# Expert gates scattered into a DRAM table by indirect transfers, in place of a one-hot gate stage

## What is computed

```python
q = (h @ w_q).reshape(B, L, PEER_HEADS, 2, PEER_HALF)
s = jnp.einsum('blhpd,pnd->blhpn', q, sub_keys).astype(jnp.float32)
top_s, top_i = lax.top_k(s, PEER_TOPK)
cand_s = top_s[..., 0, :, None] + top_s[..., 1, None, :]
cand_i = top_i[..., 0, :, None] * PEER_NKEYS + top_i[..., 1, None, :]
best_s, best_pos = lax.top_k(cand_s.reshape(B, L, PEER_HEADS, PEER_TOPK * PEER_TOPK), PEER_TOPK)
idx = jnp.take_along_axis(cand_i.reshape(B, L, PEER_HEADS, PEER_TOPK * PEER_TOPK), best_pos, axis=-1)
gate = jax.nn.softmax(best_s, axis=-1)
...
act = jax.nn.gelu(jnp.einsum('bpd,bphkd->bphk', hb, u).astype(jnp.float32), approximate=False)
coef = (act * gb).astype(hb.dtype)
return jnp.einsum('bphk,bphkd->bpd', coef, v_tab[ib])
```

## Time and profile before

| | us |
|---|---|
| median of 3 runs | 2644.88 |
| lowest, highest | 2641.59, 2645.89 |
| profiled execution | 2653.0 |
| its span, first to last instruction | 2651.1 |
| TensorE busy in the span | 2427.9 |
| VectorE busy | 1689.4 |
| ScalarE busy | 1294.4 |
| GpSimd busy | 0.4 |

### The profile page before, as it was taken

How to read it: one execution, slowest core, us unless ns; L and a number is a source line. 1 busy time by engine, 2 the same in 40 slices (tenths; PEclk the granted TensorE clock), 3 DMA queues, 4 the chain that set the end, 5 groups by cost and what they waited for, 6 DMA issues and landing times.

```text
span 2651.1 us, 47498 instructions
## 1 busy us (share of the span) xinstructions
PE 2427.9 (92%) x15508; PEld 2160.0 (81%) x15508; DVE 1689.4 (64%) x3506; ACT 1294.4 (49%) x2816; POOL 0.4 (0%) x5
## 2 busy tenths in 40 slices
PE   7989979999995799999899999989999985899998
PEld 2767779999995688888677778789999985788887
DVE  2565247888759766666225674238888769766665
ACT  1456145555558655554123422045555568655554
POOL 0000000000000000000000000000000000000000
PEclk9989989999999999999899899999999999999999
DMA  6445444555540255555332212445555530355554
GB/s 229 137 167 190 141 154 145 182 182 181 185 141 0 80 190 189 190 190 174 99 127 88 80 56 80 135 143 177 182 181 182 183 111 0 115 186 184 188 183 141
DMA packets 108500, 388.91 MB, mean 147 GB/s; under 512 B 12784, under 2 KB 15088, under 8 KB 107776
## 3 DMA queue, kind: packets, MB, share of 16 engines
q1 hardware_dynamic: 104256, 380.16, 43.1%
q10 hardware_dynamic: 4160, 7.61, 0.9%
HBM read 386.67 MB, written 1.05 MB: 146 GB/s over the span
## 4 chain that ended last, share of the span: by engine, by line
PE 83%; DVE 10%; issue 3%; ACT 2%; DVEq 0%; DMA 0%; ACTq 0%; PEld 0%; PEldq 0%
PE ps L707 19%; PE ps L1314 18%; PE ps L1308 11%; PE ps L1309 10%; PE ps L1310 10%; PE ps L1315 9%; DVE gbuf L1545 2%; DVE arena L1579 2%; PE ps L789 2%; PE ps L1000 1%; PE ps L978 1%; PE ps L1345 1%; DVE gbuf L801 0%; DMA ring<-stream 0%; PE ps L1570 0%
## 5 line engine op out<-in xcount | busy, mean ns | idle before, releaser
L1314 PE MATMUL ps<-csplit,hl 128*128 128x512 f32 x2048 | 721.2, 398 | 6.2 <-DVE hl L1611 6.2
L1308 PE MATMUL ps<-hsplit,hl 128*128 128x256 f32 x2304 | 656.3, 285 | 31.7 <-DVE hl L1385 31.7
L1309 PE MATMUL ps<-hsplit,hl 128*128 128x256 f32 x2304 | 655.5, 285 | 0.0
L1310 PE MATMUL ps<-hsplit,hl 128*128 128x256 f32 x2304 | 655.4, 284 | 0.0
L1315 PE MATMUL ps<-csplit,hl 128*128 128x256 f32 x2048 | 573.2, 280 | 0.0
L1382 ACT CAST hl<-ring 128x512 fp32r<-128x512 f32 x576 | 355.9, 621 | 388.0 <-PE ps L1310 387.7
L1385 DVE TENSOR_TENSOR hl<-ring,hl 128x512 fp32r<-128x512 f32 x576 | 397.6, 692 | 221.9 <-ACT hl L1382 189.8
L1308 PEld LDWEIGHTS ps<-hsplit,hl 128*128 128x128 f32 x2304 | 445.8, 193 | 32.8 <-ACT hl L1382 32.8
L1314 PEld LDWEIGHTS ps<-csplit,hl 128*128 128x128 f32 x2048 | 386.5, 189 | 99.6 <-issue 6.5
L707 PE MATMUL ps<-arena,ring 128*128 128x256 f32 (+2 forms) x1896 | 449.3, 397 | 15.5 <-issue 10.8
L1309 PEld LDWEIGHTS ps<-hsplit,hl 128*128 128x128 f32 x2304 | 445.7, 193 | 0.0
(11 more groups left out here) (194 smaller groups left out, 1808.7 us busy)
## 6 DMA issues: line engine op xcount, KB each, us to landing
ring<-stream SPq DMA_DIRECT2D x723, 512.0 KB, 3.3
arena<-keys ACTq DMA_DIRECT2D x2, 1024.0 KB, 4.9
gbuf<-consts ACTq DMA_DIRECT2D x1, 1120.0 KB, 5.1
arena<-xT ACTq DMA_DIRECT2D x1, 1024.0 KB, 10.3
arena<-ctxT ACTq DMA_DIRECT2D x1, 1024.0 KB, 12.7
resid<-xT ACTq DMA_DIRECT2D x1, 1024.0 KB, 8.8
out<-resid SPq DMA_DIRECT2D x1, 1024.0 KB, 3.9
gbuf<-consts ACTq DMA_DIRECT2D x1, 832.0 KB, 6.6
```

Of the source, the lines that this page charges most:

```text
L1308: pe.matmul(out_ap, w[0], m[0], start=start, stop=False)
L1309: pe.matmul(out_ap, w[1], m[0], start=False, stop=False)
L1310: return pe.matmul(out_ap, w[0], m[1], start=False, stop=stop)
L1314: pe.matmul(ps[:, bank, :], w_hi, m_both, start=start, stop=False)
```

## The change

The gates go through a table in DRAM, `gates_dram[b]`, laid out as (expert of the unit, unit, token) so that one cell of 4 bytes holds the gate of one expert and token; a unit's 128 x 256 gates are one contiguous 128 KB tile.

ScalarE's queue fills each table with zeros by 16 stores (`act_zero`): the first table's after the first norm, ahead of `con1` and `resid`, the second's ahead of the first expert layer, behind the keys. VectorE's work is regrouped in four rounds of four items. While it searches for round i, it also does the lookups and the softmax of round i - 1 (`lookup_part`, 14 steps), and ends with the numbers of the table's cells (`picks_at`). Several copies of the search are dropped, since the results are written in place. GpSimd then adds the gates into the table (`pool_scatter`): one accumulating indirect DMA for each of 256 columns of 128 tokens, with a wait for all that were sent before each head, as two heads of a token can pick the same expert.

The transposes on TensorE and the gate stage are gone. In the second-table stage SyncE loads the gate tile of a unit into `gring` (four slots), after it has waited once for all scatters, and VectorE multiplies the activations of a unit by it, two units ahead of use (`multiply`). The second table's stage starts on PSUM banks 4 to 7 while ScalarE still takes the last two units out of the others. The loops of the first-table stage are written out on VectorE and ScalarE. TensorE's loop has four units throughout.

```diff
+    gring, _ = place("gring", [P, GRING, T])
+    zeros, _ = place("zeros", [P, ZEROS])
...
+    gates_dram = {b: nc.dram_tensor(f"gates{b}", (P, P, T), F32, kind="Internal").ap() for b in (1, 2)}
...
+    hit = gring[:, :, :].rearrange("p r (c a) -> p (r c) a", a=TOPK)
...
         if n == 0:
-            eng.tensor_copy(keybuf[:, :], s_area[:, ds(i * 1024 + q * 256, 256)])
-            eng.drain()
-            for x, keys, _ in halves_of:
+            for x, keys, _ in both:
                 eng.max(topbuf[:, x, 0:8], keys)
...
         if n == 5:
-            eng.tensor_copy(index_f[:, :, ds(at, TOPK)], idxbuf[:, :, :])
...
         if n == 6:
-            eng.max(bestbuf[:, 0:8], keybuf[:, :])
-            eng.drain()
-            eng.match_replace(tmpbuf[:, :], bestbuf[:, 0:8], keybuf[:, :], NEG)
+            eng.max(best[:, at], keybuf[:, :])
         if n == 7:
-            eng.max(bestbuf[:, 8:16], tmpbuf[:, :])
-            eng.max_index(posbuf[:, 0:8], bestbuf[:, 0:8], keybuf[:, :])
+            eng.max_index(picks_pos[:, at], best[:, at], keybuf[:, :])
+            eng.match_replace(tmpbuf[:, :], best[:, at], keybuf[:, :], NEG)
...
         if n == 9:
-            eng.tensor_copy(sum_best[:, ds(at, TOPK)], bestbuf[:, :])
-            eng.tensor_copy(sum_pos[:, ds(at, TOPK)], posbuf[:, :])
+            eng.max_index(picks_pos[:, at8], best[:, at8], tmpbuf[:, :])
...
+    EXP_LAG = 3
+    def lookup_part(eng, b, i, n):
...
+        done = 4 * (b - 1) + i + 1
         if n == 0:
...
+            eng.tensor_copy(pos_f, picks_pos[:, :])
+            eng.tensor_copy(key_f, picks_key[:, :, :])
+            eng.tensor_tensor(g4, best, best[:, :, 0:1].broadcast_to([P, ITEMS, TOPK]), ALU.subtract)\
+               .then_inc(S("gates_shifted"), 1)
         if n == 1:
...
+            eng.tensor_scalar(rank1, pos_f, 1.0 / TOPK, -15.0 / 32, ALU.mult, ALU.add)
...
+        if 4 <= n < 10:
+            x, step = divmod(n - 4, 3)
...
             if step == 0:
...
+                eng.tensor_tensor(hit, rank, every, ALU.is_equal)
...
+                keys = key_f[:, x, :].rearrange("p (h o a) -> p h o a", h=ITEMS, o=1)\
...
+                eng.tensor_tensor(h4, h4, keys, ALU.mult)
             if step == 2:
...
+                eng.tensor_reduce(chosen[:, x, :], hit, AX_X, ALU.add)
+        if n == 10:
+            eng.wait_ge(S("gates_exp"), done)
+            eng.tensor_reduce(gate_sum[:, 0, :], g4, AX_X, ALU.add)
+            eng.scalar_tensor_tensor(chosen[:, 0, :], chosen[:, 1, :], float(P), chosen[:, 0, :], ALU.mult, ALU.add)
...
+            eng.scalar_tensor_tensor(chosen[:, 0, :], chosen[:, 0, :], float(T), c_("token"), ALU.mult, ALU.add)
...
+            eng.tensor_tensor(g4, g4, z, ALU.mult)
+        if n == 13:
+            eng.tensor_copy(picks_at[:, i, :], chosen[:, 0, :]).then_inc(S("picks_ready"), 1)
+        eng.drain()
...
+    def pool_scatter(pool, b):
+        cells = gates_dram[b].rearrange("j i (t o) -> (j i t) o", o=1)
+        pool.wait_ge(S(f"zeroed{b}"), 16 * (P * T // ZEROS // 4))
+        sent = (b - 1) * NT * HEADS * TOPK
+        for i in range(ROUNDS):
+            pool.wait_ge(S("picks_ready"), 4 * (b - 1) + i + 1)
+            for head in range(ITEMS // 2):
+                wait(pool, "scattered", 16 * sent)
+                for k in range(TOPK):
+                    for t in range(NT):
+                        c = (2 * head + t) * TOPK + k
+                        pool.indirect_dma_start(
+                            out=cells, out_offset=bass.IndirectOffsetOnAxis(ap=picks_at[:, i, c:c + 1], axis=0),
+                            in_=gates[:, i, c:c + 1], in_offset=None, compute_op=ALU.add,
+                            bounds_check=P * P * T - 1, oob_is_err=True).then_inc(S("scattered"), 16)
+                        sent += 1
+    def act_zero(act, b):
+        rows = gates_dram[b].rearrange("j i t -> j (i t)")
+        wide = zeros[:, :].rearrange("p (o n) -> p o n", o=1).broadcast_to([P, 4, ZEROS])
+        act.wait_ge(S("zeros_ready"), 1)
+        for n in range(P * T // ZEROS // 4):
+            act.dma_start(rows[:, n * 4 * ZEROS:(n + 1) * 4 * ZEROS].rearrange("j (o n) -> j o n", o=4), wide)\
+               .then_inc(S(f"zeroed{b}"), 16)
...
+    V_BANKS = (4, 5, 6, 7, 3, 0, 1, 2)
...
+    def multiply(dve, b, i, s):
+        at = s % GRING
+        dve.wait_ge(S(f"gates_in{at}"), i * 16 + 16 * ((b - 1) * N_IT + s // GRING + 1))
+        c = ds(i * (UB * T) + s * T, T)
+        dve.tensor_tensor(acts[:, c], acts[:, c], gring[:, at, :], ALU.mult).then_inc(S("gated"), 1)
...
+                        eng.copy(hl[:, hslot, 0, :], slot(unit)[:, part]).then_inc(S("split_hi"), 1)
                         if half == 0:
+                            eng.wait_ge(S("gated"), i * UB + ((b - 1) * P + s + 1))
                             eng.copy(csplit[:, cslot, 0, :], acts[:, c]).then_inc(S("csplit_hi"), 1)
-                        eng.copy(hl[:, hslot, 0, :], slot(unit)[:, part]).then_inc(S("split_hi"), 1)
...
+                        if first and s == 0 and half == 1:
+                            eng.wait_ge(S("u_bank_free"), banks_freed(b + 1, "wq"))
...
+                            mm = wide_passes(eng, v_bank(half * KD // 2 + n), w[0], w[1], csplit[:, cslot, :, :],
...
+                if kind == "act" and first and s == 0:
+                    take_unit(eng, b, 0, P - 2)
+                    take_unit(eng, b, 0, P - 1)
+                if kind == "dve" and not (last and s >= UB - 2):
+                    if first:
+                        eng.wait_ge(S("u_bank_free"), banks_freed(b, "u") + 4 + s + 3)
+                    elif last or s == 0:
+                        eng.wait_ge(S("u_bank_free"), banks_freed(b + 1, "wq"))
+                    multiply(eng, b, i, s + 2)
...
+        if kind == "dve":
+            for s in range(2):
+                eng.wait_ge(S("u_bank_free"), banks_freed(b, "u") + 4 + s + 1)
+                multiply(eng, b, 0, s)
...
-        with pe.Fori(0, TOPK_IT) as i:
-            for s in range(TOPK_UB):
-                u_unit("pe", pe, b, i, s, TOPK_UB)
-        for n in range(MID_UNITS):
-            u_unit("pe", pe, b, 0, MID_AT + n)
-            pe_gate_part(pe, b, n)
-        u_loop("pe", pe, b, MID_END // UB, N_IT)
...
-        with pe.Fori(0, NG // GRING) as i:
-            for n in range(GRING):
-                pe_gates(pe, b, i * GRING + n, n)
-        pe.wait_ge(S("gated"), b * (NG + GRING))
+        u_loop("pe", pe, b, 0, N_IT)
...
-        for s in range(UB):
+        for s in range(P):
             u_unit("act", act, b, 0, s, first=True)
...
+            i, n = divmod(2 * s, ROUND_SLOTS)
+            if n == 2 * EXP_LAG and 1 <= i <= ROUNDS:
+                act.wait_ge(S("gates_shifted"), 4 * (b - 1) + i)
+                act.activation(gates[:, i - 1, :], gates[:, i - 1, :], ACT.Exp).then_inc(S("gates_exp"), 1)
...
-        for g in range(HOT_AHEAD):
-            dve_hots(dve, b, g, g)
-        with dve.Fori(0, NG // GRING - 1) as i:
-            for n in range(GRING):
-                dve_hots(dve, b, i * GRING + (n + HOT_AHEAD), (n + HOT_AHEAD) % GRING)
-                dve_multiply(dve, b, i * GRING + n, n)
...
+        def between(n):
+            item, step = divmod(n, 10)
+            if item < NT * HEADS:
+                topk_part(dve, item, step)
+            i, step = divmod(n, ROUND_SLOTS)
+            if 1 <= i <= ROUNDS and step < LOOK_STEPS:
+                lookup_part(dve, b, i - 1, step)
+        for s in range(P):
+            u_unit("dve", dve, b, 0, s, extra=between)
...
+                for s in range(RING):
+                    freed(v0 + s - RING)
+                    load(v0 + s)
+                sp.wait_ge(S("scattered"), 16 * b * NT * HEADS * TOPK)
+                for s in range(GRING):
+                    load_gates(b, 0, s)
+                n1 = peer_units[v0]
+                with sp.Fori(1, N_IT) as i:
+                    for s in range(RING):
+                        sp.wait_ge(S("split_lo"), i * 2 * RING + 2 * (n1 + s + 1) - 2 * RING)
+                        u = v0 + s
+                        sp.dma_start(slot(u), stream[bass.ds(i * RING + u, 1), :, :]
+                                     .rearrange("a p n -> (a p) n")).then_inc(S(ring_full[u % RING]), 16)
+                        sp.wait_ge(S("gated"), i * UB + ((b - 1) * P + s + 1 - UB))
+                        load_gates(b, i, s)
...
+            pool.memset(zeros[:, :], 0.0).then_inc(S("zeros_ready"), 1)
+            for b in (1, 2):
+                pool_scatter(pool, b)
...
             norm_x.act(act)
             act_h1_context(act)
+            act_zero(act, 1)
             act.dma_start(con1, consts1).then_inc(S("consts_loaded"), 16)
             act.dma_start(resid[:, :, :], xT).then_inc(S("consts_loaded"), 16)
...
             act.dma_start(keys_area, keys1).then_inc(S("keys_loaded1"), 16)
+            act_zero(act, 2)
             peer_act(act, 1)
```

(65 more changed lines are left out.)

196 lines of the change are left out of this document (45 added, 151 removed).

## The result

The changed kernel takes 3363.7 us (median of 5 runs, 3351.9 to 3370.0) against 2644.9 us before (5 runs, 2640.5 to 2652.0): ratio 1.271, 95% interval 1.269 to 1.274. The profiled execution has a span of 3349.9 us against 2651.1, 698.8 more. The prediction was 2575 us, on the other side.

A forecast was written before the change was run, and what follows sets the result against it. TensorE's matmuls were taken to bound the kernel, except in the gate stage, limited by VectorE. The terms -232 + 8 + 22 + 46 + 40 + 46 = -70 gave 2575 us; range of 8 in 10: 2490 to 2960.

The forecast's parts named there:

- the price of a scatter: Time c of one GpSimd scatter in sequence, taken as 1.26 us; TensorE then waits 23 us, twice: +46 us.
- L = 256 c - 299: TensorE's wait L per block for the last scatter after the first-table stage; nothing below c = 1.17 us.
- the point of return: Scatter price at which the change stops gaining: L = 58 us, c = 1.39 us; chance of c above it 0.43.
- GpSimd becomes the bound: Slower rival: scatters cost over 1.39 us; at c = 2.0, L = 213 and 2955 us; chance 0.43, lock's 0.07 included.
- The lock: Rival: scatters written only while VectorE isn't in its split; c = 2.4, L = 315, total 3159 us; chance 0.07.
- Removed stages: Both one-hot gate stages, between first and second table, leave the path: 115.9 + 116.0 us, -232 us.
- hand-over: From first to second table, TensorE waits about 4 us for gate load, multiplies and splits, twice: +8 us.
- steady second-table stage: VectorE gains 55 us of multiplies and DMA share rises to about 0.71; TensorE covers both: 0.
- Lookups: First-table stage: lookups beside top-k steps stall TensorE 3.4 to 3.9 us in three rounds, 11 us a block: +22 us.
- Zeroing 1: First table's zero stores delay the constant loads; ScalarE's takes start near 113 us and TensorE stalls: +46 us.
- Zeroing 2: Second table's zero stores hold ScalarE ahead of the cast that opens the expert stage: +40 us, bounds 0 and 50.

The follow-up runs named there:

- e4: Changed kernel without scatters, gate loads waiting for the zeros only (all gates stay zero): 2523.1 us, ratio 0.953.
- e2: Changed kernel with the scatters writing instead of adding, descriptor space still 1024 bytes: 2804.5 us, ratio 1.058.
- e5: Changed kernel with the scatters writing instead of adding and descriptor space 4096 bytes instead of 1024: 2703.4 us, ratio 1.023.
- e1: Changed kernel with descriptor space 4096 bytes instead of 1024, nothing else: 3029.9 us, ratio 1.148.
- e8: Changed kernel with descriptor space 2048 bytes instead of 1024: 3103.5 us (one run).
- e6: Changed kernel without scatters, 1024 bytes of descriptor space, the 32 zero stores issued from GpSimd instead of ScalarE: 2467.1 us, ratio 0.933.
- e3: Changed kernel with descriptor space 4096 bytes and each adding scatter covering 64 partitions instead of 128: 2920.4 us (one run).
- e7: Changed kernel, whole result, with descriptor space 4096 bytes and the 32 zero stores issued from GpSimd instead of ScalarE: 2995.8 us, ratio 1.131.

## Why the prediction was wrong

**The step that failed** is the price of a scatter. The formula L = 256 c - 299 held to 5 us in every kernel of the table, and the point of return was well placed: from e4's 2523 it is c = (61 + 299) / 256 = 1.41, where the prediction had 1.39. But c was 1.26 by a geometric mean between the issue of one DMA, 0.34 us, and a whole latency, 4.8 us, and it measured 2.81. (That mean is in fact 1.28, which would have made the forecast 2585, still far off.) The bounds were right. The lower end was not near: 0.34 us is what ScalarE and SyncE take, and no row showed GpSimd issuing anything. Its own instruction takes 1.55 us plus 0.30 between two, so 1.85 before anything is waited for, which is above the point of return. "1024 pieces landed in 5.3 us, so that 128 are not many" was the argument against the rival; it looked at the transfers, and 1.85 of the 2.81 us were in the issuing. A range around a mean of two ends that no row picks between should have let both ends through. Spread evenly in the logarithm from 0.34 to 4.8 us, a third of the chance lies above 2.0, where the range of 8 in 10 ended, and 0.46 above the point of return.

**Which rival came.** "GpSimd becomes the bound", with c = 2.81 where I priced 2.0. Its reason (small pieces that read, add and write) was half of it: e2 and e5 put 0.63 (4096 bytes) and 1.06 us (1024) of c on the adding; the space put 0.65 on it (2.80 - 2.15). No row and no run shows a scatter at the 2.0 us on which this rival's 2955 and the top of the range (2960) rest; the means measured were 2.80 us at 1024 bytes, 2.15 at 4096 (e1) and, writing, 1.74 (e2) and 1.52 (e5). Instruction and pause are two costs: the median instruction is 1.55 us in the changed kernel, e8 and e1 alike (means of 1.59), while the pause goes from 1.13 to 0.64 and 0.50 us a scatter. The written waits of the changed kernel with nothing else running are 2.2 to 2.5 us from the end of one instruction to the start of the next.

**The lock** (VectorE holds GpSimd off, c = 2.4) did not come. With VectorE at work a scatter keeps GpSimd busy for 1.64 us (75.51 / 46), without it for 1.54 (60.16 / 39). What grows beside the stream is the pause, from 1.9 to 2.9 us in the middle.

**Removed stages, hand-over.** -232 and +8. TensorE starts 4.2 us behind the gate loads; without scatters (e4) it waited 1.4 and 1.9 us, so the hand-over itself was less than the 4 us each. (Its terms also add up to 6.5 us, not 6.8.) The steady second-table stage was covered, at a DMA share of 0.73 where 0.71 was forecast:

```profile
1300.00:1600.00 300.00, 300.00 (x1733) 262.34 (x1732) 220.05 (x434) 167.65 (x325) 0.00 (x0) 1.00 0.73 236
```

**Lookups.** Predicted 11 us a block from three stalls of 3.4 to 3.9. The waits in block 1's first table come in three groups, as forecast: TensorE waits for VectorE's and ScalarE's splits 3.8, 3.7 and 3.7 us in sum (540 to 600, 600 to 660, 660 to 720 us), no single wait over 1.6. The first wait of the stage, 3.6 us, isn't of this kind: the kernel before has it with 3.5.

**Zeroing 1.** Predicted +46, first take at 113. Timeline, ScalarE:

```profile
53.58 33.53 ACTq L1513 DMA_DIRECT2D gates<-zeros  x12
87.14 2.65 ACTq L1736 DMA_DIRECT2D gbuf<-consts  x1
89.82 1.27 ACTq L1737 DMA_DIRECT2D resid<-xT  x1
103.18 0.92 ACT L464 COPY arena<-ps 128x512 f32<-128x512 f32 x3 [49.34 <-DMA resid<-xT]
```

Four stores go out freely and twelve hold ScalarE, as the count of pieces said; the take comes at 103.18 and TensorE stands 36.7 us. The transfers ran faster than the two rates I took: 380 GB/s from 60 to 80 us, against 270 and 333.

**Zeroing 2.** Predicted 40. ScalarE is held from 376.61 to 411.3, and VectorE waits 33.91 us for its cast. TensorE's longest wait ahead of the layer grows from 13.3 to 45.2 us, so it costs 32 (waits, before and changed; ACT timeline, changed):

```profile
PE ps L1308 <- DVE hl L1385: 31.7, 4, 13.3
PE ps L1305 <- DVE hl L1379: 80.8, 23, 45.2
```
```profile
376.61 34.65 ACTq L1513 DMA_DIRECT2D gates<-zeros  x13
411.30 1.90 ACT L1604 CAST hsplit<-gbuf 128x2048 fp32r<-128x2048 f32 x1 [37.49 <-issue]
```

**Together**: -232 + 839 (TensorE's two long waits, the hand-overs in them) + 37 + 32 + 22 = +698, against 699 in the spans. The closeness is partly luck: without scatters the same terms give about -138, and e4's span is 128 shorter than before. Some 10 us stay unplaced, as much as two executions of one kernel differ here.

## What to carry to other kernels

Price an engine's first DMA work by that engine's own issue time; another queue's issue time was no bound near it here (0.34 us on ScalarE and SyncE, 1.85 us on GpSimd before any pause). The small indirect transfers of this case cost per instruction (1.41 us with 64 cells, 1.55 with 128), so count instructions times spacing against the cover before anything else: here the first table just covers 128 adding scatters, and 256 leave a wait of 254 to 422 us a block. Before giving such a design up, look for pauses at a fixed count and vary the descriptor space: here 4096 bytes instead of 1024 took 334 us off. When transfers are moved to an idle engine, ask what they now run ahead of: the zero stores on GpSimd delayed TensorE's first matmul from 9.7 to 12.9 us (e6).

## What the runs showed of the hardware

- An indirect DMA of 128 cells of 4 bytes keeps GpSimd busy for 0.97 us when it writes (e2, e5) and 1.55 us when it adds (changed kernel, e8, e1), with 0.30 us between two. With 64 cells adding still takes 1.41 us (e3).
- Adding turns 32 packets a scatter into 144 and 0.4% of the DMA engines' time into 6.7% (e2 and the changed kernel).
- The space for GpSimd's descriptors (`dynamic_dma_scratch_size`) sets after how many scatters GpSimd pauses, by count and not by time: adding, every third and seventh at 1024 bytes, every seventh at 2048, every 15th and 28th at 4096; writing, every seventh at 1024 and every 28th at 4096. A pause is 1.8 to 2.2 us when nothing else runs and up to 4.4 us beside the stream in the changed kernel. The profile lists it as "issue".
- TensorE's granted clock stood at 0.50 in the long waits of the changed kernel, when it had no matmul at all (900 to 1270 and 2600 to 2900 us). It cost little: the 3.0 us after 1285.10 had ten matmuls at a mean clock of 0.53, and the 2.9 us after them 19 at 1.00, so some 1.5 us by an estimate from these counts.
- Stores of 1 MB ran at 380 GB/s almost alone (changed kernel, 60 to 80 us), and stores and loads together at 399 to 416 (e7, 20 to 80 us).
